# A hybrid decoder step on one core: the sample compression by three sets of products in place of four, and four loads of dilated values issued at another place of the ScalarE queue

## The reference

```python
def _compress(kv, pe, w1, w2):
    n = T // CMP_STRIDE                      # 2048 / 16 = 128 chunks of 16 rows
    r = CMP_LEN // CMP_STRIDE                # 32 / 16 = 2 halves
    n_cmp = n - r + 1
    ch = kv[:, :n * CMP_STRIDE].reshape(B, n, CMP_STRIDE, 2, K, Dh)
    for half in range(r):
        proj = jnp.einsum('bncskd,scdh->bnskh', ch + pe_h, w1[:, sl])
        parts.append(proj[:, half:half + n_cmp])
    hid = jax.nn.silu(sum(parts))
    return jnp.einsum('bnskh,shd->bnskd', hid, w2)
```

## Time and profile before

| what | value |
|---|---|
| median of 3 runs | 2289.65 us |
| the profiled execution | 2288.92 us |
| its span, first to last instruction | 2287.1 us |
| PE busy | 2191.5 us (96%) |
| DVE, ACT, POOL busy | 893.4, 564.1, 646.6 us |
| chain that ended last: PE | 86% |
| TensorE's granted clock, mean | 0.992 of full speed |
| sample batches | 8 per layer, 2 layers; one period is about 36.1 us |

### The profile page before, as it was taken

How to read it: one execution, slowest core, us unless ns; L and a number is a source line. 1 busy time by engine, 2 the same in 40 slices (tenths; PEclk the granted TensorE clock), 3 DMA queues, 4 the chain that set the end, 5 groups by cost and what they waited for, 6 DMA issues and landing times.

```text
span 2287.1 us, 42944 instructions
## 1 busy us (share of the span) xinstructions
PE 2191.5 (96%) x13416; PEld 1569.2 (69%) x13416; DVE 893.4 (39%) x2336; ACT 564.1 (25%) x1372; POOL 646.6 (28%) x733
## 2 busy tenths in 40 slices
PE   7999998999999999999999999989999999999997
PEld 4545567677777777777745556767777677777776
DVE  2013763433453222336510147533344523133475
ACT  2111661211113322120211146411111233121202
POOL 0001771101143334434200037510113334333440
PEclk9999999999999999999999999999999999999999
DMA  9733026999964444544275310389999444444441
GB/s 347 255 148 92 7 78 190 277 277 276 274 231 167 172 172 182 198 190 183 106 276 202 141 61 0 105 264 278 275 284 301 179 155 188 172 172 172 177 166 42
DMA packets 130750, 424.93 MB, mean 186 GB/s; under 512 B 18337, under 2 KB 90274, under 8 KB 114082
## 3 DMA queue, kind: packets, MB, share of 16 engines
q1 hardware_dynamic: 108928, 326.01, 40.2%
q10 hardware_dynamic: 21666, 97.06, 14.6%
HBM read 412.40 MB, written 152.57 MB: 247 GB/s over the span
## 4 chain that ended last, share of the span: by engine, by line
PE 86%; issue 4%; DVE 4%; SPq 1%; POOL 1%; DMA 1%; ACT 1%; DVEq 0%; POOLq 0%; ACTq 0%
PE bank L1099 39%; PE bank L1182 14%; PE bank L1395 10%; PE bank L1568 2%; PE bank L1362 2%; PE bank L1330 2%; PE bank L1342 2%; PE bank L1464 2%; PE bank L1195 1%; PE bank L1592 1%; POOL zone L945 1%; PE bank L1519 1%; DMA ring<-in_cache_kv_cmp 1%; PE bank L1540 1%; SPq L514 1%
## 5 line engine op out<-in xcount | busy, mean ns | idle before, releaser
L1099 PE MATMUL bank<-zone,ring 128*128 128x288 f32 x1664 | 424.8, 407 | 10.3 <-DVE zone L1730 7.6
L1099 PEld LDWEIGHTS bank<-zone,ring 128*128 128x128 f32 x1664 | 314.8, 190 | 103.3 <-DVE zone L1730 13.1
L1099 PE MATMUL bank<-zone,w 128*128 128x288 f32 x1408 | 353.5, 406 | 0.0
L1182 PE MATMUL bank<-ring,hT 128*128 128x512 f32 (+2 forms) x800 | 329.7, 566 | 6.2 <-ACTq L767 4.9
L1099 PEld LDWEIGHTS bank<-zone,w 128*128 128x128 f32 x1408 | 267.5, 190 | 73.9
L1182 PEld LDWEIGHTS bank<-ring,hT 128*128 128x128 f32 (+1 forms) x800 | 147.4, 189 | 157.6 <-issue 146.6
L1395 PE MATMUL bank<-ring,w 128*128 128x128 f32 x2048 | 245.2, 279 | 10.4 <-DMA ring<-in_cache_kv_cmp 10.4
L899 POOL TENSOR_TENSOR w<-ring 128x512 f32<-128x512 f32 x72 | 93.5, 1299 | 546.3 <-PE bank L1099 309.3
L1395 PEld LDWEIGHTS bank<-ring,w 128*128 128x128 f32 x2048 | 235.5, 194 | 14.6 <-DMA ring<-in_cache_kv_cmp 10.5
L629 ACT COPY zone<-bank 128x288 f32<-128x288 f32 x72 | 28.6, 398 | 557.5 <-PE bank L1099 557.5
L1021 POOL TENSOR_TENSOR zone<-constants,stat 128x1024 f32<-128x1024 f32 x16 | 30.3, 1897 | 427.2 <-DVE stat L2089 427.2
(11 more groups left out here) (251 smaller groups left out, 2681.1 us busy)
## 6 DMA issues: line engine op xcount, KB each, us to landing
out_dil_s<-in_state_kv_dil SPq DMA_DIRECT2D x48, 2720.0 KB, 12.3
ring<-in_w_units SPq DMA_DIRECT2D x72, 1024.0 KB, 4.8
ring<-in_cache_kv_cmp SPq DMA_DIRECT2D x256, 128.0 KB, 3.1
ring<-in_cache_kv_sel SPq DMA_DIRECT2D x256, 128.0 KB, 9.9
zone<-in_batch_rows ACTq DMA_DIRECT2D x14, 2112.0 KB
zone<-in_batch_rows ACTq DMA_DIRECT2D x30, 768.0 KB, 5.6
ring<-in_w_in SPq DMA_DIRECT2D x10, 2048.0 KB, 8.1
zone<-in_batch_rows ACTq DMA_DIRECT2D x14, 1088.0 KB, 6.3
```

The costliest lines, as they stand in the source:

```text
L1099: last = mm(dst[:, 0:HALF], lhs[:, k, :], rhs(k), start=first and k == 0, stop=(k == 3), skip_group_check=True)
L1182: last = mm(dst, hT[:, k, t * P:t * P + ROWS[t]], ring[:, n % 2, k * CH:k * CH + width], start=start and k == 0, stop=stop and k == KT - 1)
```

## The change

Chunks are taken in pairs, even and odd. Of a pair, W_second · even, W_first · odd and (W_first + W_second) · (even + odd) are computed. The hidden value of an even chunk is the third less the other two, wherein the second and first halves come out as W_first · even + W_second · odd, and the hidden value of an odd chunk is W_first · odd plus W_second · even of the next pair. That makes 3 x 8 x 2 = 48 products of 128x128 with 128 columns (two heads by 64 pairs). Around them:

- GpSimd adds the two halves of the weights once a layer (`w1_sum`), and the even and odd chunks in place, twice a batch (`add_pairs`), when TensorE is done with the even ones (`h_second`).
- ScalarE keeps the first result in SBUF (`keep_second`), VectorE makes the sums and the difference (`odd_sums`, `even_sums`), and the exponential reads them from SBUF.
- The hidden chain on VectorE is interleaved for the two halves; `h_done` 1 and 2 come from `keep(0)` and `keep(1)`.
- The four loads of the next batch's dilated values move on ScalarE from the end of the batch to behind the first exponential of the compression (`next_values`); the load of the window moves ahead of the exponential of the selected scores.
- The window's scores wait for `h_sum` 2, the compressed values for `h_done` 2.
- The host lays out the raw pages with even and odd chunks apart.

```diff
-HID_BANK, FIRST_HID = (4, 5), (2, 3)
+HID_BANK, FIRST_HID = (4, 5, 7), (2, 3, 1)
@@ scalar
+            def keep_second(it, at):
+                act.wait_ge(h_second.sem, h_second.at(it, 2))
+                for s in range(2):
+                    last = copy(by_page(second[:, s, :, 0:64]), by_head(bank[at][:, s * P:(s + 1) * P]))
+                last.then_inc(h_kept.sem, 1)
...
+                def hidden_exp(it, at, between=None):
                     for s in range(2):
-                        act.wait_ge(h_full.sem, h_full.at(it, s + 1))
-                        act.wait_ge(h_done.sem, h_done.at(it, s))
...
+                        act.wait_ge(h_sum.sem, h_sum.at(it, s + 1))
+                        nc.scalar.activation(hes[s].rearrange("p (k n) -> p k n", k=2), summed[:, s], ACT.Exp, scale=-1.0,
+                                             bias=ncbias[:, s:s + 1]).then_inc(s_hexp.sem, 1)
+                        if s == 0 and between is not None:
+                            between()
...
+                    if more:
+                        act.wait_ge(win_pv.sem, win_pv.at(it, 1))
+                        load_window(act, l, b + 1)
                     act.wait_ge(s_pad.sem, s_pad.at(it, 1))
...
-                    if more:
-                        act.wait_ge(win_pv.sem, win_pv.at(it, 1))
-                        act.wait_ge(od_full.sem, od_full.at(it, 1))
-                        load_dilated_v(act, l, b + 1)
-                        load_last_v(act, l, b + 1)
-                        load_window(act, l, b + 1)
...
+                def next_values(b):
+                    act.wait_ge(od_full.sem, od_full.at(l * NB + b, 1))
+                    load_dilated_v(act, l, b + 1)
+                    load_last_v(act, l, b + 1)
+
                 with act.Fori(0, NB - 1) as b:
                     batch(b, True)
-                    hidden_exp(l * NB + b + 1, HID_BANK)
+                    keep_second(l * NB + b + 1, HID_BANK[0])
+                    hidden_exp(l * NB + b + 1, HID_BANK, lambda: next_values(b))
@@ gpsimd
+                        nc.gpsimd.tensor_tensor(w1_sum, w1[:, :, 0:8, :], w1[:, :, 8:16, :], ALU.add).then_inc(w1_add.sem, 1)
...
+                def add_pairs(it):
+                    for s in range(2):
+                        pool.wait_ge(h_second.sem, h_second.at(it, s + 1))
+                        pool.sem_inc(waits_taken_pool, 1)
+                        nc.gpsimd.tensor_tensor(rawt[:, :, s, :, 0, :], rawt[:, :, s, :, 0, :], rawt[:, :, s, :, 1, :],
+                                                ALU.add).then_inc(raw_sum.sem, 1)
@@ tensor, batch
-                        compress(0, 0, 3, HID_BANK[0])
+                        second_of_even(0, HID_BANK)
...
-                        compress(0, 3, 11, HID_BANK[0])
+                        second_of_even(1, HID_BANK)
+                        first_of_odd(0, HID_BANK)
...
-                        compress(0, 11, 16, HID_BANK[0])
-                        compress(1, 0, 16, HID_BANK[1])
-
-                compress(1, 8, 16, FIRST_HID[1])
+                        first_of_odd(1, HID_BANK)
+                        both_of_sum(it + 1, 0, HID_BANK)
+                        both_of_sum(it + 1, 1, HID_BANK)
@@ vector
+                    dve.wait_ge(h_kept.sem, h_kept.at(it, 1))
+                    dve.wait_ge(h_first.sem, h_first.at(it, 2))
+                    added = odd_sums(0)
+                    even_sums(0, added)
+                    added = odd_sums(1)
+                    inverse(0)
+                    even_sums(1, added)
+                    keep(0)
+                    inverse(1)
+                    keep(1)
```

More of the change, by code:

```diff
@@ L290, in build, with by_page, by_head @@
         ptd = part(stg_at + 1344, 3, P)
+        at_sums = 6656 + KA + KB
+        second = part(at_sums, 2, 2, 65)
+        summed = part(at_sums + 260, 2, 2, P)
+        hes = [he, part(stg_at + 1728, 256)]
+        assert at_sums + 772 <= W and stg_at + 1984 <= 21900
+        def by_page(v):
+            return v.rearrange("p k (g m) -> p k g m", m=4)
+        def by_head(v):
+            return v.rearrange("p (g k m) -> p k g m", k=2, m=4)
         gb, gm = part(m + 2496, 192, rows=low), part(m + 2048, 192)
@@ L303, in build @@
         raw = ring[:, 0, :]
-        rawt = raw.rearrange("p (g s k i n) -> p g s k i n", g=NPG, s=2, k=2, i=8)
+        rawt = raw.rearrange("p (g s i e x) -> p g s i e x", g=NPG, s=2, i=8, e=2)
         kvsel = ring[:, 1, :].rearrange("p (g f) -> p g f", g=NPG)
@@ L1387, in chunk_outputs, with second_of_even, first_of_odd, both_of_sum @@
                 mm(bank[6][:], vcp[:], p_ptc, start=False, stop=True, skip_group_check=True)
-            def compress(s, lo, hi, at):
-                out = bank[at][:, 0:258].rearrange("p (k n) -> p k n", k=2)
-                for j in range(lo, hi):
-                    first = 1 if j < 8 else 0
-                    for k in range(2):
-                        last = mm(out[:, k, first:first + P], w1[:, s, j, :], rawt[:, :, s, k, j % 8, :],
-                                  start=(j == 0 and k == 0), stop=(j == 15 and k == 1), skip_group_check=True)
-                if hi == 16:
-                    last.then_inc(h_full.sem, 1)
+            def second_of_even(s, at):
+                out = bank[at[0]][:, s * P:(s + 1) * P]
+                for j in range(8):
+                    last = mm(out, w1[:, s, 8 + j, :], rawt[:, :, s, j, 0, :], start=(s == 0 and j == 0), stop=(j == 7),
+                              skip_group_check=True)
+                last.then_inc(h_second.sem, 1)
+            def first_of_odd(s, at):
+                out = bank[at[1]][:, s * P:(s + 1) * P]
+                for j in range(8):
+                    last = mm(out, w1[:, s, j, :], rawt[:, :, s, j, 1, :], start=(s == 0 and j == 0), stop=(j == 7),
+                              skip_group_check=True)
+                last.then_inc(h_first.sem, 1)
+            def both_of_sum(it, s, at):
+                out = bank[at[2 * s]][:, 2 * P:3 * P]
+                if s == 0:
+                    pe.wait_ge(h_kept.sem, h_kept.at(it, 1))
+                pe.wait_ge(raw_sum.sem, raw_sum.at(it, s + 1))
+                pe.sem_inc(waits_taken_pe, 1)
+                for j in range(8):
+                    last = mm(out, w1_sum[:, s, j, :], rawt[:, :, s, j, 0, :], start=(s == 1 and j == 0), stop=(j == 7),
+                              skip_group_check=True)
+                last.then_inc(h_full.sem, 1)
             def prompt_steps(l, g, first, last, ends):
@@ L2027, in hidden_batch, with odd_sums @@
                     horder = Order(ch_h, it)
-                    for s in range(2):
+                    def odd_sums(s):
+                        y = summed[:, s].rearrange("p k (g m e) -> p k g m e", m=4, e=2)
+                        first = by_head(bank[at[1]][:, s * P:(s + 1) * P])
+                        V.tensor_tensor(y[:, :, :, :, 0], first, by_page(second[:, s, :, 0:64]), ALU.add).then_inc(horder.sem, 1)
+                        V.tensor_tensor(y[:, :, :, :, 1], first, by_page(second[:, s, :, 1:65]), ALU.add)
+                        return horder.next()
@@ L2031, in hidden_batch, with keep @@
                         dve.wait_ge(horder.sem, horder.next())
[L2032 removed]
+                        V.reciprocal(hes[s], hes[s]).then_inc(horder.sem, 1)
                         dve.wait_ge(horder.sem, horder.next())
+                    def keep(s):
                         V.scalar_tensor_tensor(
[L2035 to L2037 removed]
```

75 lines of the change are left out of this document (47 added, 28 removed).

## The result

| | median, us | range, us | runs |
|---|---|---|---|
| before | 2289.39 | 2289.12 to 2290.79 | 4 |
| after | 2458.06 | 2445.82 to 2469.1 | 4 |

The ratio is 1.073 (95% interval 1.068 to 1.079). The prediction said 2387 us and a range of 2312 to 2425: the direction and the place are right, the size is 71 us short, and the time lies outside the range. The profiled execution took 2465.07 us, its span 2463.2 us, with a mean granted clock of 0.928 (0.992 before).

The account below looks back on a forecast made before the run. TensorE was taken as the bound, transfers close behind. Per transition -3.7 (products) + 9.4 (late keys) + 1.5 (clock) = +7.2 us, 14 times +100.8, first batches -4: 2386 us profiled, median 2387 us, range 2312 to 2425.

Parts of the forecast that it names:

- Bound and place: Steady batches: TensorE is the bound, transfers close behind; a new wait for the last dilated keys at the late dilated scores.
- Products: Compression products on TensorE: 16 fewer a batch, 1536 records instead of 2048, saving 3.7 us in each of 14 transitions.
- The stall's size: Late dilated scores: last keys land at T0+17.2, so the scores start there instead of at T0+7.8, 9.4 us later.
- T0: Time mark in a batch's timeline: the start of its first dilated scores, from which the other times are counted.
- the upper bound: Last keys' landing at the latest: window's longest landing (16.6) and extra bytes at half rate, given as T0+19.5, 11.7 us later.
- The stall's cause: ScalarE's queue: the last dilated keys stand behind the dilated values, as ring descriptors are consumed in order; landing was 5.0 us.
- The window's 14.8 us: Landing of the 512 KB window transfer behind the values on ScalarE before the change, used to price the keys' delay.
- The fit that the prediction set beside it: Last keys' transfer: 2.0 us plus bytes at 436 GB/s, 3.8 us for 768 KB, an estimate that meant no stall.
- The clock: TensorE after the new stall: half clock, recovery 3.9 us as in one earlier case, 1.5 us lost (between 0 and 1.9).
- First batches: Each layer's first batch: raw-page wait 3 us less, a 4.6 us gap may lose 1 us of clock; sum -2 us a layer.
- The second bound: DMA engines, busy 0.95 of a batch: as a rival, a transition gains only 1.8 us, 2260 us; chance 0.03.
- The hidden chain: VectorE's chain for the hidden values: second half done 1.5 us later, priced at 0.9 us a batch, forecast to show nowhere.

Follow-up runs that it names:

- the products alone: The changed kernel with ScalarE's five loads (dilated values and window) put back to the end of the batch, keeping the three products: 2277.76 us, 0.995.
- the reordered version: The three products with loads put back, hidden chain reordered on TensorE and VectorE: 2284.3 us; with 1152 KB of each batch's loads left out, 2238.44 us.
- short rows: The values' 22 KB rows loaded as 8, 8 and 6 KB: three products with loads put back 2266.85 us; also with the chain reordered 2257.82 us.

## Why the prediction was wrong

- *Bound and place: right.* TensorE led, the transfers were close behind, and the new wait is the one named, at the late dilated scores, 14 times.
- *Products: right.* 1536 records, and -3.7 us a batch is borne out by the mean period of 41.8 us once the clock is kept up.
- *The stall's size: right, though its sum was not clean.* Scores at T0+16.5 for T0+17.2, 8.7 us later than before for 9.4. The terms named give T0+16.7+0.8 = T0+17.5, and the upper bound comes to T0+20.1, not T0+19.5; with it the range would have ended at 2433 us and still missed.
- *The stall's cause: wrong in one word.* "It stands behind the values in the same queue" was the reason; on another queue the landing is the same (13.3 us). The window's 14.8 us, from which the number came, contained the true cause too, the bytes in front, so the number survived; for a wrong reason that was luck. The fit that the prediction set beside it from the Trainium skill, page "DMA: Bandwidth & Descriptors", section "Anatomy of one DMA", is headed there as one for the path of GpSimd, and ScalarE issued these loads.
- *The clock: the step that failed.* "Half of the rest is lost: 1.5 us" measured 6.1 us a transition, 14 x 4.6 = 64 us of the 71 us missing. The 3.9 us of recovery were one case, read where TensorE ran compression products back to back; behind the new stall the clock came back after 6.5 to 22.5 us. The range took its upper bound (1.9 us) from the same row and so couldn't hold the time. Why the recovery differs so much stays open: behind the new stall come transposes and products with short waits for ScalarE, but that is the same in the transition with 6.5 us and in that with 17, and no run put other work there.
- *First batches: wrong by about 3 us a layer.* From the first batch's T0 to the second's are 41.0 and 40.5 us in the two layers, 43.6 and 43.1 before: 2.6 us less, where the products and this term together said 5.7. The wait for raw pages did not shrink (10.0 us for two, 10.4 before), and the gap of 4.6 us at the layer's start, which the prediction named, came in full. This is read from the rows; no run was made for it. With the clock's 64 us and the 10 us by which the 14 stalls were shorter than forecast, these 6 us account for 60 of the 71; the rest is within the 23 us by which the runs of the changed kernel differ.
- *The second bound.* "The DMA engines' 0.95 x 36 = 34.3 us can't be squeezed" was a rival with a chance of 0.03. It did not set the changed kernel's time, but it is what bounds the products alone: a period of 34 to 36 us, and in the reordered version 33.0 once bytes are taken away.
- *The hidden chain.* Priced at 0.9 us and hidden. In the run with the products alone the scores that choose the pages ran at T0+7.1 for T0+5.4: 1.7 us. In the changed kernel they lie ahead of the stall and are hidden by it. Reordering brought a gain with short rows (9 us) and none with long ones.

## What to carry to other kernels

Ask for a large load where the time until its use covers all bytes asked for with it at the rate the trace shows, and don't expect another queue to pass it: in a batch whose DMA engines are busy for 0.95 of the time, a transfer's place in time is its price. Price a new wait of TensorE of some microseconds by the clock as well, and don't take the recovery from one row: like waits with like work behind them gave 6.5 to 22.5 us here. A run with idle products in the wait tells what the clock costs. When work is taken from the leading engine, work out first the period at which the next resource is full.

## What the runs showed of the hardware

- The granted clock came back 6.5 to 22.5 us after work resumed behind 14 waits of 5.4 to 7.2 us (17 us in the one shown), and stood at half for at least 18 us behind one of 1.98 us, with TensorE at work for all but 0.45 us of the 18.
- It also fell with no wait for a transfer: in the run with the products alone, between 440 and 446, behind waits on VectorE of 0.74, 0.42 and 1.01 us, the last of them ending at 439.79:

```profile
436.00:440.00 4.00, 2.57 (x46) 1.56 (x35) 3.43 (x10) 0.77 (x4) 0.00 (x0) 1.00 1.10 357
...
442.00:444.00 2.00, 2.00 (x32) 0.99 (x32) 1.25 (x8) 0.00 (x0) 0.00 (x0) 0.50 1.10 354
444.00:446.00 2.00, 1.34 (x24) 0.93 (x15) 0.51 (x2) 0.88 (x3) 1.87 (x2) 0.82 1.10 348
```

- A transfer of 768 KB, first in a queue of its own, took 13.3 us beside one of 2112 KB asked for 2.6 us earlier on another queue, and 4.9 us when it was ahead of it.
- With the DMA engines' share at 1.00 the rate in the transition (445.8 to 462.3) was 252 GB/s, where the stretch from 504 to 506 above shows 370. In the run with the products alone, short rows raised it from 283 to 292 GB/s (441 to 511 us).
